# Up projection of the conv-gated FFN: pair results written back to PSUM, two plain pairs in front, products stored by SyncE

## The reference, cut to what matters

```python
def conv_gated_ffn(h, w_up, conv_w, conv_b, w_down):      # h [1024, 1024], w_up [1024, 8192], w_down [4096, 1024]
    u = h @ w_up
    u_pad = jnp.pad(u, ((0, 0), (2, 0), (0, 0)))
    u = conv_b + sum(conv_w[j] * u_pad[:, j:j + S] for j in range(3))   # along the tokens
    gate, val = jnp.split(u, 2, axis=-1)
    return (jax.nn.gelu(gate, approximate=True) * val) @ w_down
...
    x = x + rms_norm(mix, norm_mix_post)
    f = conv_gated_ffn(rms_norm(x, norm_ffn_pre), ...)
    x = x + rms_norm(f, norm_ffn_post)                     # x2, which the second block reads
```

## Time and profile before

| | us |
|---|---|
| median of 3 runs (2607.18 to 2617.12) | 2611.32 |
| the profiled execution, its own time | 2615.84 |
| its span | 2614.0 |
| TensorE busy / VectorE / GpSimd / ScalarE | 2420.3 / 1467.0 / 1391.7 / 953.2 |
| mean granted TensorE clock | 0.961 of full speed |

### The profile page before, as it was taken

How to read it: one execution, slowest core, us unless ns; L and a number is a source line. 1 busy time by engine, 2 the same in 40 slices (tenths; PEclk the granted TensorE clock), 3 DMA queues, 4 the chain that set the end, 5 groups by cost and what they waited for, 6 DMA issues and landing times.

```text
span 2614.0 us, 46105 instructions
## 1 busy us (share of the span) xinstructions
PE 2420.3 (93%) x17630; PEld 1906.5 (73%) x17630; DVE 1467.0 (56%) x1824; ACT 953.2 (36%) x1432; POOL 1391.7 (53%) x782
## 2 busy tenths in 40 slices
PE   8999989999978989889999899989999999998788
PEld 5777679987856767767777787777777877773357
DVE  4476775544585656656655524454336066666564
ACT  3233532232343434334444212222135224556641
POOL 3322100014668777777777689769667444440045
PEclk9999999999979999999999999999899999999899
DMA  4211000003413323222221445655332111122033
GB/s 145 76 33 33 25 8 4 5 19 100 127 64 97 96 96 96 92 94 92 92 89 64 165 165 184 221 175 193 105 129 73 45 49 46 46 76 85 1 105 121
DMA packets 103111, 230.71 MB, mean 88 GB/s; under 512 B 7320, under 2 KB 42392, under 8 KB 102808
## 3 DMA queue, kind: packets, MB, share of 16 engines
q1 hardware_dynamic: 74528, 152.06, 18.2%
q10 hardware_dynamic: 28408, 76.24, 8.4%
HBM read 189.47 MB, written 38.80 MB: 87 GB/s over the span
## 4 chain that ended last, share of the span: by engine, by line
PE 58%; DVE 16%; POOL 8%; ACT 7%; issue 6%; DMA 2%; ACTq 1%; DVEq 1%; POOLq 0%; SPq 0%
PE ps L741 13%; PE ps L1350 5%; PE ps L837 5%; PE ps L1230 4%; DVE cg L145 4%; POOL slot_lo L611 4%; PE ps L1232 4%; PE ps L1233 4%; PE ps L1373 2%; DVE cv L145 2%; ACT cg L145 2%; POOL w_lo L606 2%; PE ps L1017 1%; ACT ab L145 1%; PE ps L1007 1%
## 5 line engine op out<-in xcount | busy, mean ns | idle before, releaser
L559 POOL TENSOR_TENSOR w_hi<-w_raw,small 128x1024 fp32r<-128x1024 f32 x156 | 307.0, 1968 | 786.0 <-PE ps L741 341.9
L562 POOL TENSOR_TENSOR w_lo<-w_raw,w_hi 128x1024 fp32r<-128x1024 f32 x156 | 431.1, 2764 | 12.2
L741 PE MATMUL ps<-x_hi,w_hi 128*128 128x512 f32 x608 | 231.6, 404 | 12.3 <-DVE x_lo L145 7.9
L611 POOL TENSOR_TENSOR slot_lo<-scr,slot_hi 128x512 fp32r<-128x512 f32 x124 | 209.1, 1692 | 43.0 <-ACT slot_hi L145 42.7
L741 PE MATMUL ps<-x_lo,w_hi 128*128 128x512 f32 x608 | 225.6, 394 | 0.0
L741 PE MATMUL ps<-x_hi,w_lo 128*128 128x512 f32 x608 | 225.4, 394 | 0.0
L1190 PE MATMUL ps<-x_hi,slot_hi 128*128 128x512 f32 x248 | 109.3, 441 | 71.7 <-DVE c_val L145 67.8
L1190 PE MATMUL ps<-t_hi,slot_hi 128*128 128x512 f32 x372 | 146.7, 394 | 6.4 <-DVE t_lo L145 3.6
L741 PEld LDWEIGHTS ps<-x_hi,w_hi 128*128 128x128 f32 x608 | 115.4, 191 | 47.4 <-DVE x_lo L145 12.8
L1191 PE MATMUL ps<-t_lo,slot_hi 128*128 128x512 f32 x372 | 145.0, 390 | 0.0
L1192 PE MATMUL ps<-t_hi,slot_lo 128*128 128x512 f32 x372 | 144.9, 390 | 0.0
(11 more groups left out here) (359 smaller groups left out, 6361.8 us busy)
## 6 DMA issues: line engine op xcount, KB each, us to landing
w_raw<-wall SPq DMA_DIRECT2D x187, 512.0 KB, 3.5
f_raw<-f_spill SPq DMA_DIRECT2D x64, 512.0 KB, 4.3
f_spill<-cg ACTq DMA_DIRECT2D x32, 512.0 KB, 2.8
v_raw<-wall SPq DMA_DIRECT2D x31, 512.0 KB, 3.5
ada_w<-wada ACTq DMA_DIRECT2D x24, 512.0 KB, 3.9
fill_spill<-stage ACTq DMA_DIRECT2D x24, 256.0 KB, 2.0
x_in<-xT ACTq DMA_DIRECT2D x8, 512.0 KB, 8.8
x<-xT ACTq DMA_DIRECT2D x8, 512.0 KB, 4.4
```

The costliest lines, as they stand in the source:

```text
L559: nc.gpsimd.tensor_tensor(w_hi[:, u, :, :], w_raw[:, u, :, :], sm["one"].unsqueeze(2).to_broadcast([P, KT, P]), ALU.mult).then_inc(S("w_hi ...
L562: nc.gpsimd.tensor_tensor(w_lo[:, u, :, :], w_raw[:, u, :, :], w_hi[:, u, :, :].bitcast(F32), ALU.subtract).then_inc(S("w_split"), 1)
L611: tt_p(slot_lo[i][:, :, :], src, slot_hi[i][:, :, :].bitcast(F32), ALU.subtract).then_inc(later("s_lo")[0], 1)
L741: last = mm(ps[:, 2 * u + h, :], w[:, u, k, :], x[:, k, h * 512:(h + 1) * 512], start=(k == 0 and w is w_hi and x is hi), stop=(k == KT - ...
```

## The change

It has these parts.

1. **Results in PSUM.** `c_gate` and `c_val` are gone. P0 is copied to a small tile `p1`, the partial sum of `c22` goes to `w1`, and the four quadrants are written back to PSUM so that gate and value each fill two neighbouring banks. First tap and the two others read PSUM. TensorE may start P0 of a pair once the gated product of the pair two before is made (`prod`), in place of `c11` of the pair before.
2. **Store by SyncE.** `cg` becomes two tiles. SyncE, behind the weight loads of each pair, waits for the product and stores it.
3. **Order of the lists.** ScalarE: `val_conv` and `first_out` stand ahead of the GELU; `second_out` of the next pair is the last in the step and slot 0 follows it. VectorE: `c21` ahead of the gate taps, and `c22` of the next pair at the end, behind the gated product. GpSimd keeps its order within a pair.
4. **Two plain pairs.** Pair 1 is plain too (30 Strassen pairs are left). Its token half 0 is computed ahead of pair 0's, and its weights are loaded and split a second time for half 1. GpSimd splits two more tiles ahead of the residual additions and two after them; `across_second` moves from GpSimd to VectorE.
5. **Down projection.** Steps 2 and 3 get tiles of their own for their activations. `down_out` of two of the four upper banks moves to ScalarE. The residuals of half 0 are done two per step over four steps, and one pair of squares per step. Ten in place of six feature blocks of head tiles stand ahead of the wait for the last copies.

```diff
+UP_ORDER = (2, 3, 0, 1, 2, 3)
...
-        c_gate = at("c_gate", [P, T], 36)
-        c_val = at("c_val", [P, T], 37)
-        cg = at("cg", [P, T], 26)
+        p1 = at("p1", [P, 512], 36)
+        w1 = at("w1", [P, 512], 36, off=UNIT // 2)
+        cg = [at("cg0", [P, T], 26), at("cg1", [P, T], 37)]
...
-            return ps[:, ((4, 6, 7, 5), (0, 1, 2, 3))[q][b], :]
+            return ps[:, 4 * q + (3, 0, 1, 2)[b], :]
...
+            def store(p):
+                sp.wait_ge(S("prod"), p + 1)
+                sp.dma_start(f_dram[p], cg[p % 2][:, :] if p else cg_first[:, :]).then_inc(later(f"f_out{p % 2}")[0], 16)
...
+            for p in range(4, N_PAIR):
+                sp.wait_ge(*later("s_sum", 4 * (p - 3)))
+                gate_in(p)
+                sp.wait_ge(*later("s_lo", 5 * (p - 3)))
+                val_in(p)
+                store(p - 3)
...
-            with pool.Fori(G_OUT // 2, G_FFN // 2 + 1) as i:
+            with pool.Fori(G_OUT // 2, G_FFN // 2 + 2) as i:
                 for u in range(2):
                     split(2 * i + u, u, i + 1)
...
+            first_sum(2, 0, 1)
+            slot_low(2, 0, scr[:, 0, 0, :, :])
             pool.wait_ge(S("x_lo_done"), 24)
             for k in range(4):
                 across(k)
...
+            for u in range(2):
+                split(G_FFN + 4 + u, u, (G_FFN + 4) // 2 + 1)
+            third_sum(2, 0, 1)
+            gate_low(2, 0)
...
             def up_pair(p, q, first=False):
-                pe.wait_ge(*later("a_lo", p))
-                if not first:
-                    pe.wait_ge(*later("st_c", 5 * p - 9))
+                pe.wait_ge(*later("a_lo", p - 1))
+                pe.wait_ge(S("prod"), p - 1)
...
                 if ada is not None:
...
-                second_out(p, q)
+                slot_high(p + 1, 0, scr[:, 1 - q, 0, :, :])
                 slot_high(p + 1, 1, scr[:, 1 - q, 0, :, :])
                 slot_high(p + 1, 2, scr[:, 1 - q, 1, :, :])
                 slot_high(p + 1, 3, scr[:, 1 - q, 0, :, :])
-                gate_conv(p)
+                gate_conv(p, q, turn - 1)
                 slot_high(p + 1, 4, v_raw[:, 1 - q, 4:8, :])
-                gate_gelu(p)
-                val_conv(p)
+                val_conv(p, q)
                 first_out(p + 1, 1 - q)
+                gate_gelu(p, q)
                 if not last:
                     gate_high(p + 2, q, turn)
-                    slot_high(p + 2, 0, scr[:, q, 0, :, :])
-                store(p)
+                    second_out(p + 1, 1 - q)
...
             def up_step(p, q, ada=None):
-                c22(p, q)
                 if ada is not None:
...
                 c12(p, q)
-                gate_taps(p)
                 c21(p, q)
-                val_taps(p)
+                gate_taps(p, q)
+                val_taps(p, q)
                 c11(p + 1, 1 - q)
-                gated_product(p)
+                gated_product(p, q)
+                c22(p + 1, 1 - q)
...
-                if 36 <= n < 39:
-                    for k in range(3 * n - 108, min(KT, 3 * n - 105)):
-                        residual(0, k)
+                if 36 <= n < 40:
+                    residual(0, 2 * n - 72)
+                    residual(0, 2 * n - 71)
+                if 38 <= n < 42:
+                    half_pair("b", 2, n - 38)
```

More of the change, by code:

```diff
@@ L525, in _ @@
+            for p in (2, 3):
+                sp.wait_ge(S("w_split"), G_FFN + p + 3)
+                gate_in(p)
+            store(0)
+            sp.wait_ge(*later("f_out0", 16))
+            val_in(3)
+            for p in range(4, N_PAIR):
+                sp.wait_ge(*later("s_sum", 4 * (p - 3)))
+                gate_in(p)
+                sp.wait_ge(*later("s_lo", 5 * (p - 3)))
+                val_in(p)
+                store(p - 3)
+            store(N_PAIR - 3)
             for n in range(N_PASS * N_STEP):
@@ L538, in _ @@
                 if n < N_STEP:
-                    sp.wait_ge(*later("f_out", 16 * (2 * j + 2)))
+                    for q in range(2):
+                        sp.wait_ge(*later(f"f_out{q}", 16 * (j + 1)))
                 sp.dma_start(f_part(f_raw, n), f_dram[2 * j:2 * j + 2, :, hc(h)].rearrange("k p t -> p k t"))\
-                    .then_inc(later(f"f_in{u}")[0], 16)
+                    .then_inc(later(f"f_in{f_slot(n)}")[0], 16)
+                if n in (1, 3):
+                    store(N_PAIR - 2 + n // 2)
             for g in range(G_IN2, N_POS):
@@ L1133, in out_half, with up_part @@
                 gemm(g, g % 2, x_hi, x_lo, parts=("x_lo_done", 8) if h == k == 0 else None, hs=(h,), k0=k0, k1=k1)
-            def up_half(h, u, k0=0, k1=KT):
-                gemm(G_FFN + u, u, x_hi, x_lo, parts=("x_lo_done", 16 + 8 * h), hs=(h,), k0=k0, k1=k1, whole=(h == 1))
+            def up_part(u, b, h, k0=0, k1=KT):
+                for k in range(k0, k1):
+                    pe.wait_ge(S("x_lo_done"), 16 + 8 * h + k + 1)
+                    for w, x in ((w_hi, x_hi), (w_hi, x_lo), (w_lo, x_hi)):
+                        last = mm(ps[:, b + h, :], w[:, u, k, :], x[:, k, hc(h)],
+                                  start=(k == 0 and w is w_hi and x is x_hi), stop=(k == KT - 1 and w is w_lo),
+                                  skip_group_check=True)
+                return last
             pe.wait_ge(S("inv_used"), 4)
@@ L2701, in gate_taps, with val_taps @@
-            def gate_taps(p):
+                dve.wait_ge(*later("st_mm", 7 * p - 7))
+                tt(up_bank(q, 3), u2[:, :], up_bank(q, 3), ALU.add).then_inc(later("st_c")[0], 1)
+            def gate_taps(p, q):
                 dve.wait_ge(S("conv_a"), 2 * p + 1)
-                taps(cg, c_gate, dve.snap(2 * p)).then_inc(S("taps"), 1)
-            def val_taps(p):
+                taps(cg[q], pair(4 * q), dve.snap(2 * p)).then_inc(S("taps"), 1)
+            def val_taps(p, q):
                 dve.wait_ge(S("conv_a"), 2 * p + 2)
-                taps(cv, c_val, dve.snap(2 * p + 1))
@@ L2723, in _ @@
             dve.wait_ge(S("conv_a"), 1)
-            taps(cg0, pair(0), 0).then_inc(S("gemm_evac"), 1)
+            taps(cg_first, pair(0), 0).then_inc(S("gemm_evac"), 1)
+            dve.wait_ge(S("conv_a"), 2)
+            taps(cv_first[0], pair(2), 1).then_inc(S("gemm_evac"), 1)
+            for k in range(4):
+                across_second(k)
+            dve.wait_ge(S("gelu"), 1)
+            tt(cg_first[:, :], cg_first[:, :], cv_first[0][:, :], ALU.mult).then_inc(S("prod"), 1)
+            for k in range(4):
+                across_low(1, k)
             for k in range(4):
@@ L2727, in _ @@
             for k in range(4):
-                across_low(1, k)
-            dve.wait_ge(S("conv_a"), 2)
-            taps(cv0, pair(2), 1).then_inc(S("gemm_evac"), 1)
-            dve.wait_ge(S("gelu"), 1)
-            tt(cg0[:, :], cg0[:, :], cv0[:, :], ALU.mult).then_inc(S("prod"), 1)
-            for k in range(4):
                 across_low(2, k)
-            c11(1, 0)
+            c11(2, 0)
+            dve.wait_ge(S("conv_a"), 3)
+            taps(cg[1], pair(4), 2).then_inc(S("gemm_evac"), 1)
             for k in range(4):
                 across_low(3, k)
+            c22(2, 0)
+            dve.wait_ge(S("conv_a"), 4)
+            taps(cv_first[1], pair(6), 3).then_inc(S("gemm_evac"), 1)
+            dve.wait_ge(S("gelu"), 2)
+            tt(cg[1][:, :], cg[1][:, :], cv_first[1][:, :], ALU.mult).then_inc(S("prod"), 1)
             def up_step(p, q, ada=None):
-                c22(p, q)
                 if ada is not None:
@@ L2795, in shifted_low @@
                     ALU.add, ALU.subtract).then_inc(S("x_lo_done"), 1)
-            for n in range(2, 4 * N_STEP):
+            for n in range(4, 4 * N_STEP):
                 f_low(n)
@@ L2812, in _ @@
                     half_pair("a", 2, 3)
-                    for d in range(4):
+                    for d in range(2):
                         down_out(1, d)
```

401 lines of the change are left out of this document (215 added, 186 removed).

## The result

The changed kernel takes 2502.14 us (median of 4 runs, 2499.57 to 2506.09) against 2612.56 before (2607.18 to 2617.12): a ratio of 0.958, 95% interval 0.9556 to 0.9603. Forecast were 2492 and a range of 2470 to 2548. The profiled execution of after took 2499.57 us with a span of 2497.4, so between the two profiled executions the gain is 2614.0 - 2497.4 = 116.6 us, and the sum had 119; between the medians it is 110.4.

The account below looks back on a forecast made before the run. The loop was taken as set by a queue position on ScalarE. Gains 84 + 13 + 6.5 + 12 + 3 = 119 us, against the profiled execution 2497, with the runs' median 4.5 lower 2492; range 2470 to 2548.

Parts of the forecast that it names:

- The loop: Pairs 4 to 31: from 22.2 to 19.2 us per pair, 84 us gained, bounds 89 and 62.
- The formula: Pair loop: the period is the larger of 19.0 and (16.3 + L) / 2, which gave 18.05.
- L: Pair loop: chain from P3's end to P5 of the next pair, 19.8 us; loop free while under 21.8.
- the likeliest case: Pair loop: taps with one input in PSUM stop colliding with GpSimd and take 1.28; chance 0.66.
- The second case: Pair loop, rival "Collisions stay": taps at 2.06, period 20.0, loop gain 62, time 2514; chance 0.17.
- a queue position on ScalarE: Old pair loop: ScalarE's copy for `c22` stood behind the store, so TensorE idled 2.69 us, then ran at half clock.
- The start: Up to pair 4: a gain of 13 us, 22 without P5's wait, 3 with 10 more of VectorE.
- So pair 4 begins near 830: Start: pair 2 begins at 781, its P5 waits to about 804, so pair 4 begins near 830, not 843.19.
- Down projection: Down projection to step 63: 6.5 us from its first steps and 12 from the spread residuals, 18.5 in all.
- Steps 31 to 42: Down projection where three residuals a step load VectorE, 13 lost: 12 us back (4 to 15), ScalarE copies included.
- The first steps: Down projection: step 2's wait and half clock go with own tiles and spread taps, 6.5 us (3 to 8).
- The end: After step 63: wait of 4.75 mostly covered, but the norm moves by 1.7 only: 3 us (1.5 to 6).

Follow-up runs that it names:

- run 1: Changed kernel with the stores of pairs 2 to 29 started by ScalarE again, ahead of `second_out` of the next pair: 2544.96 us, ratio to before 0.9721.
- run 6: Changed kernel with three needless VectorE additions more in each pair, ahead of `c11`: 2527.01 us, ratio to before 0.9676.
- run 3: Changed kernel without the matrix-vector product in the pair loop: 2496.87 us, ratio to before 0.9553.
- run 4: Changed kernel without the matrix-vector product, and with the quadrants written to SBUF tiles and read there by the taps: 2524.84 us, ratio to before 0.9648.
- Run 2: Kernel before with only the stores of pairs 1 to 29 moved to SyncE, from the one tile `cg`: 2583.0 us, ratio 0.9882.
- Run 11: Changed kernel, start rearranged: ScalarE's P0 copy of pair 2 earlier, fourth activation sum's high parts last, its low parts on GpSimd: 2494.01 us, ratio to before 0.9544.
- run 7: Changed kernel with three residuals of half 0 in one step again and the squares to match: 2506.45 us, ratio to before 0.9588.
- run 8: Changed kernel with the store of the last product two loads later in SyncE's list: 2500.77 us, ratio to before 0.957.
- 9: Kernel before with the store on SyncE and the new list order, quadrants in SBUF, one `cg`: 2568.83 us, ratio 0.9836.

## Why the prediction was right, and where not

**The loop: right, in size and cause.** Forecast 19.2 per pair and 84 us, measured 19.14 and 86.2. The wait ahead of P5 went, and run 1 brings it back with the store alone. The formula held within 0.3 per pair: with the L of run 6, 23.0, it gives 19.6, and 19.95 was measured. But the term that goes into it was too small: L was taken as 19.8, and the trace puts it at 21.4, from P3's end of pair 3 at 831.26 to `w` of pair 4 at 852.67. Ahead of it were 0.9 for a slot that collides with the matrix-vector sum (2.17 where 1.28 was taken) and some 0.7 of small starts on ScalarE. Of the reserve of 2.0 (21.8 less 19.8) 1.6 was not there; the loop is free by 0.4 us, and one pair in four still waits 0.3 to 0.7 (run 3, without the sum, has none).

**Collisions: the likeliest case was right.** Taps ran at 1.28. The second case gave 62 for a loop with collisions, 20.0 per pair; run 4 made it, without the matrix-vector product, and measured 19.90, though with three taps hit and not four.

**The store as the single cause: overstated.** The prediction read the loop as set by "a queue position on ScalarE". Run 2 shows that this position alone is worth 1.05 of the 3.08 us per pair. Behind it stood `first_out`, the collisions and the order, which only the whole change takes away. The term of the loop was right because it was made from the chain of the changed kernel, not from the wait of the old one.

**The start: 13 forecast, 3.8 measured.** Restart 749.2 (750), pair 2 at 780.66 (781) and the wait ahead of P5 to 807.0 (804) came as worked out. The step that failed is "So pair 4 begins near 830". It charged nothing for half clock behind that wait (P5 and P6 took 7.2, not 5.4), and missed that pair 3's weight sums cannot start before the product of pair 1 at 811.7: they share its memory. So `first_out` of pair 3 comes late:

```profile
826.85 0.47 PE L1265 MATMUL ps<-t_hi,slot_hi 128*128 128x512 f32 x1 [4.38 <-ACT p L149]
```

That is 3.0 + 1.8 + 4.4 with 1.8 of half clock behind it, 11.0 in all, over the 828.4 that 804 and the paces of the prediction give. Run 11 shows VectorE's list to be what holds the product, and the product to be what `first_out` follows.

**Down projection: 18.5 forecast, 16.1 measured, and that with some luck.** Steps 31 to 42 gave 12.7, as forecast (12), though not by the load of three residuals alone, as argued: run 7 gives that 4.6. The first steps gave 2.0 in place of 6.5, since the wait at step 2 went and a new one came at step 4. The prediction had SyncE's queue in its list for the loop, but not here: the store of the last product stands ahead of the loads of steps 4 and 5 (run 8). The other 1.4 lie for the most part in steps 8 and 9, which differ between profiles of kernels that agree there: runs 1 and 3, with the down projection of the changed kernel, take 381.2 for this stage in place of 377.4, which would be a gain of 12.3.

**The end: 3 forecast, 10.5 measured.** The term said that the norm behind the sums moves by 1.7 only. From the start of step 63 TensorE's column sums start 12.75 us on, and 14.57 before, which is the 1.8. But the spreading of their result, the next thing the norm needs, follows 7.30 behind in place of 12.39:

```profile
1765.63 0.27 PE L801 MATMUL ps<-cst,pairs_l 128*128 128x1 f32 x1 [0.21 <-DVE f_acc L149]
...
1772.93 0.29 PE L809 MATMUL ps<-cst,small 128*128 128x128 f32 x1
```

and in the kernel before the spreading stands at

```profile
1885.97 0.27 PE L759 MATMUL ps<-cst,small 128*128 128x128 f32 x1
```

Behind the wait of 4.75 TensorE had done the 32 sum instructions at half clock, 3.4 us for 16 of them in place of 1.8, which gives 3.3; and 9 matmuls of head blocks now stand behind the sums in place of 15, which gives 1.8. With the 1.8 ahead of the sums that makes 6.9, and it repeats: from step 63 to the spreading the changed kernel and all runs on it take 19.1 to 20.1, the kernel before and runs 2 and 9 take 27.0 to 27.1. The step that failed is "the norm behind it moves by the 1.7 only": it left out the half clock behind the old wait and the fewer blocks. The remaining 3.6 cannot be told from variation: from the spreading to the end the first take 719.5 to 728.6, the others 727.0 to 730.4.

## What to carry to other kernels

Sum the chain of the changed loop, from one late event to the same event a turn later, and compare it with what the bounding engine needs; the wait that the profile names is only the first of several that stand one behind the other, and taking it away alone gave a third. Where VectorE and GpSimd share a loop, try an operand of VectorE in PSUM in place of SBUF: here it took the collisions of the taps away on both engines (1.28 in place of 2.06, and 1.30 in place of 2.1 to 2.3). After each edit look at every queue that the moved step now stands in, also where the loop ends: here the store was free in 28 pairs and cost 4.6 us behind the last.
